# Attention units with the keys' two parts stacked, sample values as wide products, and the passages before both attentions re-ordered

## The chip, the cores and the metric

One core of a Trainium2 chip runs the whole kernel. The metric is the device time of one execution in microseconds (us); the kernel is timed in several runs, and the median counts. TensorE (PE) is the matrix engine, VectorE is DVE, ScalarE is ACT, GpSimd is POOL, and SyncE (SP) issues most of the DMAs.

## The reference

The reference is one inference step of a two-layer decoder, for a prompt of 512 tokens and for 8 sample tokens, each of which has 256 cached tokens behind it. Layer 0 runs dilated window attention (A, 8 heads of 64) beside gated linear attention (B, 4 heads, keys of 64 and values of 128). Layer 1 runs sparse attention (C, 16 query heads on 4 key heads), where an indexer picks 128 keys for a query. Every layer ends with a SwiGLU feed-forward part and a gated input embedding. Everything is float32.

```python
def ab_output(oa, ob, bog, li, prm):
    gate = jax.nn.silu(bog).reshape(*lead, B_HEADS, B_DV)
    ob = rmsnorm(ob, prm['b_out_norm'][li]) * gate
    o = jnp.concatenate([oa..., ob...], axis=-1)
    return o @ prm['w_out_ab'][li]
# A and C: QK-norm, scores + T5 bias, softmax over the keys of a dilated window (A)
s = jnp.einsum('btngd,btknd->btkng', qg, kg).reshape(bx, t, k, h) + bias
s = jnp.where(valid[..., None], s, -jnp.inf)
# C: the keys come from
score = jnp.where((key_pos[None, :] <= t[:, None])[None], index_scores(iq, iw, ik), -jnp.inf)
_, idx = lax.top_k(score, topk)
# every layer's end
x = x + (jax.nn.silu(hn @ w_ff1) * (hn @ w_ff3)) @ w_ff2
x = x + jax.nn.sigmoid(rmsnorm(x, g_ple) @ w_ple_gate) * (p_l @ w_ple_proj)
```

The kernel doesn't gather keys. It computes scores against all keys up to the end of the query block and adds a bias row that is very negative where a key is not allowed. In C the choice of the indexer is added as a mask of 0 and a very negative number.

## The kernel before, in words

Activations lie transposed: features on the 128 partitions, 520 token columns (512 of the prompt, 8 of the sample). A float32 product is made from rounded parts: `x = hi + lo`, and `hi*hi + lo*hi + hi*lo` are three matrix products at the fast rate. ACT makes the high part by a copy into a rounded type, POOL or DVE subtracts it to get the low part. Weights go by SP's DMA into a ring `w_raw`, ACT makes `w_hi` (L1315), POOL makes `w_lo` (L499).

The program on PE runs in this order: the input products of A and B (`products_in(0, ...)`), attention A, output products and feed-forward (`ffn(0)`), the input products of C, attention C, `ffn(1)`. Every engine has its own program in the order of the source; semaphores join them. No scheduler changes the order.

`attention` (PE L763 to L811, ACT L1387, DVE L1806) runs over units, one per pair of heads p, head of the pair `par`, and query block `qb`: 32 units in A, 64 in C. A unit of block qb is 128 x (128, 256, 384 or 512) scores. In step i of the loop PE makes the scores of unit i (L776: `q_hi*k_hi`, `q_hi*k_lo`, `q_lo*k_hi`, preceded in C by an addition of the mask, L774), turns unit i-3 (L785, transposes) and multiplies unit i-4 with the values (L797). DVE adds the bias while it leaves the accumulator and finds the largest (L1817), ACT takes the exponential, DVE scales by the sum (L1825), ACT copies the turned block. A head has 64 features, half of the 128 rows. So the tile `q_hi` or `q_lo` of one head holds the head in 64 rows and zeros in the other 64 (`zero_half`, by ACT), and the 128-row key tile holds the keys of both heads of the pair; the zeros cancel the other head. POOL makes these query tiles while attention runs (`split`/`place_a` L589 to L597 in A, `place_q_part` L653 in C).

Between the units lies other work, called from `between(i)`. In A (PE `sample_a`, L1100) it is the attention of the 8 sample tokens, one token in a step: scores against the cache at the steps `SCORES_A` (L1084: four products of 64 weight columns with 257 moved columns), values at the steps `VALUES_A` = 26 to 34 (L1096: eight products per token, each with 128 columns of the cached values as weights and two columns moved), the product for B's sample output (L1072: 16 products of two columns, before step 0's end), and the head norms of B (L1049).

The passage from products to attention: before unit 0 of A, PE transposes V (`attention_v` L1035, L1039) and DVE copies it out (L2027), ACT and DVE split the keys (L1587, L2024), POOL splits the queries and the keys of the next pair, and ACT and POOL split the weights of the feed-forward's first block (`high`, `low`), which stand in their queues ahead. Unit 0 waits for the last input block's accumulators to be free (`free_a`), since it uses the same banks. Before unit 0 of C, DVE splits the keys (L2169), makes the three masks from the top-k result (L2173), the sample's mask (L2175), and copies the causal block into the mask of query block 0 (L2176). PE waits for all of them.

## Time and profile before

| what | value |
|---|---|
| runs | 1574.65, 1575.99, 1582.1 us |
| median | 1575.99 us |
| the profiled execution's own time | 1581.09 us |
| its span in the trace | 1579.0 us |
| PE busy | 1532.3 us, 97 % |
| products of A and B | 0 to 201 us |
| passage and attention A | 201 to 321.9 us |
| ffn(0) | to 857 us |
| products of C | to 956.6 us |
| passage and attention C | 956.6 to 1082.7 us |
| ffn(1) | to the end |

### The profile page before, as it was taken

Reading aid. Unit: us, or ns where it says so; the run is one execution under the profiler, and the core shown is the slowest. Engines: PE = TensorE matmul, PEld = TensorE weight load, DVE = VectorE, ACT = ScalarE, POOL = GpSimd, SP = SyncE. Lnnn points to the kernel's source line nnn. Section 1 sums busy time; section 2 is a strip of 40 time slices with the busy share of each in tenths; the row PEclk is TensorE's granted clock in tenths of the full one; section 3 lists DMA queues with packets and bytes.
Section 4 is the critical chain, followed back from the end, with each engine's and each line's share of the span. In section 5 each row is a group of like instructions: output and inputs, shape, how many; then the busy total and the mean of one; then the engine's idle time right before and its main releaser. Section 6 shows DMA issues by size and latency. Waiting matters only on the chain.

```text
span 1579.0 us, 31089 instructions
## 1 busy us (share of the span) xinstructions
PE 1532.3 (97%) x12240; PEld 1477.4 (94%) x12240; DVE 684.8 (43%) x1172; ACT 657.3 (42%) x1094; POOL 682.5 (43%) x349
## 2 busy tenths in 40 slices
PE   7999989999999999999999998999999999999998
PEld 6999967999999999999989787999999999999998
DVE  4044446245443434221361696765633434432224
ACT  4242645324334343232463555653434343432234
POOL 3654643033444444444346465211444444444443
PEclk9999979689999999999999998999999999999999
DMA  5222433122332232333223321121322233323323
GB/s 171 88 95 63 142 116 113 67 67 81 94 91 87 87 93 93 94 106 93 93 86 119 106 77 68 56 86 43 92 82 92 93 93 93 93 94 95 105 93 121
DMA packets 52837, 146.92 MB, mean 93 GB/s; under 512 B 5485, under 2 KB 18057, under 8 KB 52250
## 3 DMA queue, kind: packets, MB, share of 16 engines
q1 hardware_dynamic: 50346, 137.17, 28.1%
q10 hardware_dynamic: 2416, 8.72, 1.5%
q8 instruction: 50, 0.82, 0.2%
q14 instruction: 25, 0.20, 0.0%
HBM read 139.11 MB, written 6.76 MB: 92 GB/s over the span
## 4 chain that ended last, share of the span: by engine, by line
PE 93%; DVE 4%; ACT 1%; issue 1%; DMA 0%; SPq 0%; ACTq 0%; DVEq 0%
PE PS L703 73%; PE PS L797 4%; PE PS L776 3%; DVE act_lo L1797 2%; PE PS L785 2%; PE PS L719 1%; PE PS L1096 1%; PE PS L1084 1%; PE PS L886 1%; PE PS L774 1%; PE PS L1162 1%; PE PS L1231 0%; DVE pp L1911 0%; PE PS L1072 0%; PE PS L1250 0%
## 5 line engine op out<-in xcount | busy, mean ns | idle before, releaser
L499 POOL TENSOR_TENSOR w_lo<-w_raw,w_hi 128x1024 fp32r<-128x1024 f32 x217 | 534.9, 2465 | 794.6 <-ACT w_hi L1315 794.6
L703 PE MATMUL PS<-act_hi,w_hi 128*128 128x260 f32 x2544 | 727.4, 286 | 14.5 <-POOL w_lo L499 10.0
L703 PE MATMUL PS<-act_lo,w_hi 128*128 128x260 f32 x2544 | 720.2, 283 | 0.0
L703 PE MATMUL PS<-act_hi,w_lo 128*128 128x260 f32 x2544 | 719.8, 283 | 0.0
L1315 ACT ACTIVATE w_hi<-w_raw 128x1024 fp32r<-128x1024 f32 x217 | 230.1, 1060 | 708.3 <-PE PS L703 704.6
L703 PEld LDWEIGHTS PS<-act_hi,w_hi 128*128 128x128 f32 x2544 | 480.5, 189 | 28.2 <-issue 21.3
L703 PEld LDWEIGHTS PS<-act_lo,w_hi 128*128 128x128 f32 x2544 | 480.9, 189 | 0.4
L703 PEld LDWEIGHTS PS<-act_hi,w_lo 128*128 128x128 f32 x2544 | 481.1, 189 | 0.0
L703 PE MATMUL PS<-h_hi,w_lo 128*128 128x260 f32 x704 | 198.8, 282 | 0.0
L703 PE MATMUL PS<-h_hi,w_hi 128*128 128x260 f32 x704 | 198.6, 282 | 0.0
L703 PE MATMUL PS<-h_lo,w_hi 128*128 128x260 f32 x704 | 198.5, 282 | 0.0
L703 PEld LDWEIGHTS PS<-h_hi,w_hi 128*128 128x128 f32 x704 | 132.6, 188 | 0.0
L703 PEld LDWEIGHTS PS<-h_lo,w_hi 128*128 128x128 f32 x704 | 132.3, 188 | 0.0
L703 PEld LDWEIGHTS PS<-h_hi,w_lo 128*128 128x128 f32 x704 | 132.2, 188 | 0.0
L1872 DVE TENSOR_TENSOR h_lo<-tmp,h_hi 128x520 f32 x44 | 83.8, 1905 | 40.1 <-ACT h_hi L1455 40.1
L1877 DVE TENSOR_TENSOR x<-PS,x 128x520 f32<-128x520 f32 x16 | 11.2, 700 | 176.5 <-PE PS L703 176.5
L1797 DVE SCALAR_TENSOR_TENSOR act_lo<-x,vecs,act_hi 128x520 fp32r<-128x520 f32 x48 | 74.3, 1567 | 24.4 <-ACT act_hi L1326 24.3
L1864 DVE TENSOR_TENSOR tmp<-PS,sq 128x520 f32<-128x520 f32 x44 | 30.8, 700 | 103.8 <-ACT sq L1451 103.8
L1404 ACT ACTIVATE tmp<-PS 128x128 f32<-128x128 f32 (+1 forms) x96 | 41.5, 433 | 77.3 <-PE PS L785 76.0
L1868 DVE TENSOR_TENSOR tmp<-PS,tmp 128x520 f32<-128x520 f32 x44 | 30.8, 700 | 95.4 <-PE PS L703 95.4
L1788 DVE TENSOR_TENSOR sqsum<-sqsum,sq 128x520 f32<-128x520 f32 x48 | 56.3, 1172 | 20.0 <-ACT sq L1321 19.0
L1862 DVE TENSOR_TENSOR tmp<-PS,nrs 128x520 f32<-128x520 f32 x44 | 30.8, 700 | 67.3 <-PE PS L703 67.3
(329 smaller groups left out, 1870.3 us busy)
## 6 DMA issues: line engine op xcount, KB each, us to landing
w_raw<-in_w SPq DMA_DIRECT2D x217, 512.0 KB, 3.5
kcA<-in_cache_k SPq DMA_DIRECT2D x8, 512.0 KB, 4.5
biasC<-scratch_rows SPq DMA_DIRECT2D x12, 256.0 KB
x<-in_xT SPq DMA_DIRECT2D x4, 520.0 KB, 5.9
out_y<-x SPq DMA_DIRECT2D x8, 260.0 KB, 4.5
vcA<-in_cache_v SPq DMA_DIRECT2D x4, 512.0 KB, 6.1
kcC<-in_pool_k SPq DMA_DIRECT2D x16, 128.0 KB, 2.5
vcC<-in_pool_v SPq DMA_DIRECT2D x16, 128.0 KB, 2.1
```

The source lines that it names most:

```text
L499: pool.tensor_tensor(w_lo[:, s, :], w_raw[:, s, :], w_hi[:, s, :].bitcast(F32), ALU.subtract).then_inc(S("w_lo"), 1)
L703: mm = pe.matmul(PS[:, 2 * place + half, 0:HALF], w[:, s, j * P:(j + 1) * P], r[:, c, cols], start=first and n == 0 and i == 0, stop=last ...
L776: mm = pe.matmul(PS[:, i % 2, 0:W], q_of[part][par][:, p % 2, qb * P:(qb + 1) * P], k[:, k_chunk(p), 0:W], start=n == 0 and not masked, st ...
L785: mm = pe.transpose(PS[:, 2 + i % 2, kb * P:(kb + 1) * P], ps[i % 3][:, kb * P:(kb + 1) * P], ident)
L797: mm = pe.matmul(PS[:, 4 + p % 2, qb * P:(qb + 1) * P], v_of(p, par, kb), pt[:, i % 2, kb * P:(kb + 1) * P], start=i % 8 == 0, stop=i % 8 ...
L1315: act.activation(w_hi[:, s, :], w_raw[:, s, :], ACT.Copy).then_inc(S("w_hi"), 1)
L1404: act.activation(pt[:, i % 2, 0:W], PS[:, 2 + i % 2, 0:W], ACT.Copy).then_inc(S("t_c"), 1)
L1788: dve.tensor_tensor(sqsum[:], sqsum[:], sq[:, m % 2, :], ALU.add).then_inc(S("ssum"), 1)
L1797: dve.scalar_tensor_tensor(act_lo[:, c, :], x[:, c, :], vecs[:, g:g + 1], act_hi[:, c, :].bitcast(F32), ALU.mult, ALU.subtract).then_inc(S ...
L1862: dve.tensor_tensor(halves(tmp[:, 1, :]), slot(0), halves(nrs[:]), ALU.mult).then_inc(S("f_a"), 1)
L1864: dve.tensor_tensor(halves(tmp[:, 1, :]), slot(0), halves(sq[:, 0, :]), ALU.mult).then_inc(S("free_v"), 1)
L1872: dve.tensor_tensor(h_lo[:, bass.ds(f, 1), :], tmp[:, 0:1, :], h_hi[:, bass.ds(f, 1), :].bitcast(F32), ALU.subtract).then_inc(S("h_lo"), 1)
```

## The change

It has four parts.

**Merged keys.** The key tile of head `par` now holds only that head: the high part in its own 64 rows and the low part in the other 64 (`act_hi` for par 0, `act_lo` for par 1). `q_hi` is copied into both halves (the second copy is called the twin), so one product gives `q_hi*k_hi + q_hi*k_lo`, and the second, with `q_lo` and zeros, gives `q_lo*k_hi`. Each of the 96 units has two score products instead of three. ACT's zeroing of `q_hi` goes; POOL gets one more copy per head (64 x 512), the key split is done by halves: two copies and two subtractions instead of one.

**Sample values of A.** The probabilities are scattered into a zeroed tile `pzA` (POOL zeroes, ACT scatters) that serves as weights of 64 columns; the cached values are moved, 512 columns at a time: two products per token, all into one accumulator, then one for the token's own value. DVE copies the result out at step 32 and four products of 16 columns pick each head's part at step 33. The tokens stand at steps 22, 23, 24, 26, 27, 28, 30, 31.

**Masks of C.** Query block 0 has no mask product: the causal part stands in the bias rows, whose right part is set to the very negative number by a memset instead of a product (`bias_rows`, L1931). PE waits for the mask of a query block at its first unit, not for all before unit 0. The sample's mask goes to DVE step 6.

**The passages.** Attention A makes scores in banks 2 and 3 and turns in 0 and 1, so unit 0 waits for one input block less. V is transposed in steps 0 and 1; the last head sum stands at step 2, B's sample output at steps 3 and 4, B's norms 3 to 4 steps later. The last block's weight splits leave the passage: `last_high` at ACT's step 6 (A) or 4 (C), `last_low` behind POOL's pair 1. The DVE steps for the sample's queries stand ahead of the state update.

```diff
-        NORMS_A = (4, 7, 11, 15, 18)
-        VALUES_A = (26, 27, 28, 29, 30, 32, 33, 34)
+        NORMS_A = (7, 10, 14, 18, 20)
+        VALUES_A = (22, 23, 24, 26, 27, 28, 30, 31)
+        def score_bank(base, i):
+            return (2 if base == BASE_A else 0) + i % 2
...
-                    low(n + (b0 + 2), (b0 + like) % 2)
+                    final = like == IN[l]["n"] - 1
+                    if not final:
+                        low(n + (b0 + 2), (b0 + like) % 2)
...
+            def split_q(pair, par):
+                hi, twin, lo, t = place_a(pair, par)
+                split_high(t, hi, twin)
+                split_low(hi, lo, t, "A_st")
+            def split_k(pair, par):
+                k = (act_hi, act_lo)[par]
+                hi, t = k[own[par], 4 + pair % 2, 0:SEQ], yA[own[par], Y_K + pair, 0:SEQ]
+                split_high(t, hi)
+                split_low(hi, k[other[par], 4 + pair % 2, 0:SEQ], t, "k_split")
...
+                elif part == 1:
+                    pool.tensor_copy(qC[0][par][other[par], p % 2, :], q).then_inc(S("C_st"), 1)
...
-                    if masked:
-                        pe.matmul(PS[:, i % 2, 0:W], identR[:], maskC[:, qb, 0:W], start=True, stop=False)
-                    for n, (part, k) in enumerate(((0, act_hi), (0, act_lo), (1, act_hi))):
+                    by_mask = masked and qb > 0
+                    if by_mask:
+                        if i < QB:
+                            pe.wait_ge(S("topk"), 1 + qb)
+                        pe.matmul(PS[:, score_bank(base, i), 0:W], identR[:], maskC[:, qb, 0:W], start=True, stop=False)
+                    k = (act_hi, act_lo)[par]
+                    for part in range(2):
+                        mm = pe.matmul(PS[:, score_bank(base, i), 0:W], q_of[part][par][:, p % 2, qb * P:(qb + 1) * P],
+                                       k[:, k_chunk(p), 0:W], start=part == 0 and not by_mask, stop=part == 1)
...
-            pe.wait_ge(S("free_a"), AB_BLOCKS + 2)
+            pe.wait_ge(S("free_a"), AB_BLOCKS + 1)
...
-                for t in range(4):
-                    for kb in range(2):
-                        c = t * NS + b
-                        mm = pe.matmul(PS[:, 7, 256 + 2 * c:258 + 2 * c], value_place(b)[:, kb, t * P:(t + 1) * P],
-                                       ptsA[:, kb, c:c + 33:32], start=kb == 0, stop=kb == 1)
+                for kb in range(2):
+                    c = P * b + 64 * kb
+                    mm = pe.matmul(PS[0:64, 7, :], pzA[:, c:c + 64], value_place(b)[:, kb, :],
+                                   start=b == 0 and kb == 0, stop=False)
...
+                if i < 2:
+                    attention_v(2 * i)
+                    attention_v(2 * i + 1)
+                elif i == 2:
+                    last_head_sum()
+                elif i < 5:
+                    sample_out_b(i - 3)
...
+            low_keys(0)
             for qb in range(1, QB):
                 dve.tensor_scalar(maskC[:, qb, 0:W], ...).then_inc(S("topk"), 1)
-            dve.tensor_scalar(sc8[:], wk8[:], GONE, NEG, ALU.not_equal, ALU.mult).then_inc(S("d_mask"), 1)
-            dve.tensor_copy(maskC[:, 0, 0:P], causal[:, SEQ - P:SEQ]).then_inc(S("topk"), 1)
+            low_keys(1)
+            dve.wait_ge(S("topk"), QB)
```

In the rows of the program's order, the first name after the arrow is the weights' or the first operand, the last figure the moved shape, and the brackets hold the semaphores that the instruction waits for. PE at the start of attention A, before: L1039 is the second half of V's transposes, L776 are scores, L1072 is B's sample output.

```order
L1039 MATMUL PS<-const,yA 128x128 [waits y_rs,A_v]
L1039 MATMUL PS<-const,yA 128x128 x3
L1039 MATMUL PS<-const,yA 128x128 [waits y_rs,A_v]
L1039 MATMUL PS<-const,yA 128x128 x3
L776 MATMUL PS<-act_hi,q_hiA 128x128 [waits k_split,A_st,t_x,A_zq,free_a]
L776 MATMUL PS<-act_lo,q_hiA 128x128
L776 MATMUL PS<-act_hi,q_loA 128x128
L1072 MATMUL PS<-qz,s 128x2 [waits A_v,s_new,s_qz]
L1072 MATMUL PS<-qz,s 128x2 x15
L776 MATMUL PS<-act_hi,q_hiA 128x256 [waits t_x]
L776 MATMUL PS<-act_lo,q_hiA 128x256
```

After, where L812 are scores and L1073 transposes V:

```order
L812 MATMUL PS<-act_hi,q_hiA 128x128 [waits k_split,A_st,t_x,A_zq,free_a]
L812 MATMUL PS<-act_hi,q_loA 128x128
L1073 MATMUL PS<-const,yA 128x128 [waits s_new,y_rs]
L1073 MATMUL PS<-const,yA 128x128 x3
L1073 MATMUL PS<-const,yA 128x128 [waits s_new,y_rs]
L1073 MATMUL PS<-const,yA 128x128 x3
L812 MATMUL PS<-act_hi,q_hiA 128x256 [waits t_x]
L812 MATMUL PS<-act_hi,q_loA 128x256
L1073 MATMUL PS<-const,yA 128x128 [waits A_v]
L1073 MATMUL PS<-const,yA 128x128 x3
L1073 MATMUL PS<-const,yA 128x128 [waits A_v]
L1073 MATMUL PS<-const,yA 128x128 x3
```

The 16 transposes, and their waits, now stand behind the scores of units 0 and 1, and B's sample output has left this place for steps 3 and 4.

PE at one step with a sample token's values, before (L785 turns, L797 multiplies by values, L1096 are the sample's values):

```order
L776 MATMUL PS<-act_hi,q_hiA 128x384 [waits t_x]
L776 MATMUL PS<-act_lo,q_hiA 128x384
L776 MATMUL PS<-act_hi,q_loA 128x384
L785 MATMUL PS<-const,sq 128x128 [waits t_c,t_n]
L785 MATMUL PS<-const,sq 128x128 x3
L797 MATMUL PS<-tmp,rs 128x128 [waits t_c]
L797 MATMUL PS<-tmp,rs 128x128 x2
L1096 MATMUL PS<-nrs,vcA 128x2 [waits values0,sm_pnc]
L1096 MATMUL PS<-nrs,vcA 128x2 x7
```

The same kind of step after (L821 turns, L833 multiplies by values, L1128 are the sample's values):

```order
L812 MATMUL PS<-act_lo,act_hi 128x384 [waits t_x]
L812 MATMUL PS<-act_lo 128x384
L821 MATMUL PS<-const,pA 128x128 [waits t_c,t_n]
L821 MATMUL PS<-const,pA 128x128 x3
L833 MATMUL PS<-tmp,vstA 128x128 [waits t_c]
L833 MATMUL PS<-tmp,vstA 128x128 x2
L1128 MATMUL PS<-vcA,yA 64x512 [waits values0,b_ln,sm_ptc]
L1128 MATMUL PS<-vcA,yA 64x512
```

Three score products have become two, and the eight products of two moved columns have become two of 512 columns.

DVE from the end of the top-k search to unit 0 of C, before (L2169 splits the keys, L2173 and L2175 make masks, L2176 copies the causal block, L1817 adds the bias of the first unit):

```order
L2169 TENSOR_TENSOR act_lo<-yC,act_hi 128x2x512 [waits k_hi,dve_chain]
L2173 TENSOR_SCALAR maskC<-xC 128x256
L2173 TENSOR_SCALAR maskC<-xC 128x384
L2173 TENSOR_SCALAR maskC<-workC 128x512
L2175 TENSOR_SCALAR sc<-wk 8x257
L2176 CAST maskC<-const 128x128
L1817 ISA xC,statC<-PS,biasC 128x128 [waits bias00,t_s]
```

After (L2227 are the halves of the key split, L2233 the masks, L1866 the bias of the first unit):

```order
L2227 TENSOR_TENSOR act_hi<-yC,act_hi 64x2x512 [waits k_hi,dve_chain]
L2233 TENSOR_SCALAR maskC<-xC 128x256
L2233 TENSOR_SCALAR maskC<-xC 128x384
L2233 TENSOR_SCALAR maskC<-workC 128x512
L2227 TENSOR_TENSOR act_lo<-yC,act_lo 64x2x512 [waits k_hi]
L1866 ISA xC,statC<-PS,biasC 128x128 [waits bias00,t_s,topk]
```

Two splits of 64 rows take the place of one, the sample's mask and the causal block have gone from here, and the first bias waits for the three masks.

## Rows read from the trace of the kernel before

**Rows 1.** Page: busy time of the span by engine; granted clock in 40 slices.

```profile
PE 1532.3 (97%) x12240; PEld 1477.4 (94%) x12240; DVE 684.8 (43%) x1172; ACT 657.3 (42%) x1094; POOL 682.5 (43%) x349
...
PEclk9999979689999999999999998999999999999999
```

**Rows 2.** Windows: stretch, length; PE, PEld, DVE, ACT, POOL busy; PEclk, DMA share, GB/s.

```profile
201.00:226.00 25.00, 18.95 (x91) 16.47 (x90) 15.05 (x33) 13.46 (x30) 15.13 (x16) 0.75 0.27 109
226.00:271.00 45.00, 43.76 (x242) 30.95 (x241) 26.80 (x72) 23.94 (x70) 14.68 (x16) 0.95 0.45 139
271.00:288.00 17.00, 16.43 (x123) 15.60 (x123) 8.78 (x40) 8.41 (x26) 0.00 (x0) 0.90 0.17 50
289.00:322.00 33.00, 33.00 (x152) 32.24 (x151) 6.05 (x18) 6.37 (x15) 0.00 (x0) 0.50 0.14 49
322.00:326.00 4.00, 4.00 (x19) 4.00 (x20) 1.90 (x7) 0.23 (x1) 0.00 (x0) 0.50 0.00 0
965.00:1083.00 118.00, 116.34 (x844) 107.26 (x843) 74.52 (x272) 72.41 (x220) 29.48 (x30) 0.97 0.20 65
```

**Rows 3.** Timeline of PE in attention C: start, duration, engine, line, operation, tiles, shapes.

```profile
968.25 0.31 PE L774 MATMUL PS<-maskC,identR 128*128 128x128 f32 x1
968.39 0.27 PE L776 MATMUL PS<-act_hi,q_hiC 128*128 128x128 f32 x1
968.50 0.27 PE L776 MATMUL PS<-act_lo,q_hiC 128*128 128x128 f32 x1
...
971.17 0.34 PE L776 MATMUL PS<-act_hi,q_hiC 128*128 128x384 f32 x1
971.35 0.34 PE L776 MATMUL PS<-act_lo,q_hiC 128*128 128x384 f32 x1
...
973.04 0.40 PE L776 MATMUL PS<-act_hi,q_hiC 128*128 128x512 f32 x1
973.28 0.39 PE L776 MATMUL PS<-act_lo,q_hiC 128*128 128x512 f32 x1
```

**Rows 4.** Chain of waits in attention A: start, duration, engine, line, instructions.

```profile
237.72 1.88 PE PS L1084 x8
...
284.31 1.68 PE PS L1096 x16
...
297.30 3.21 PE PS L1096 x16
```

**Rows 5.** Timeline of all engines in the passage to attention A.

```profile
196.97 1.32 POOL L512 TENSOR_TENSOR yA<-yA,rs 128x520 f32<-128x520 f32 x1
200.24 1.04 PE L719 MATMUL PS<-sq,const 128*128 128x260 f32 x4
201.12 1.04 PE L1039 MATMUL PS<-const,yA 128*128 128x128 f32 x8
205.40 0.30 PE L776 MATMUL PS<-act_hi,q_hiA 128*128 128x128 f32 x1 [1.58 <-DVE act_lo L2024]
206.50 6.90 PE L1072 MATMUL PS<-qz,s 128*128 128x2 f32 x32 [0.57 <-DVE vtokA L2027]
225.75 1.11 PE L1080 MATMUL PS<-sbA 33*64 33x257 f32 x2
```

**Rows 6.** Timeline of DVE in the passage to attention C.

```profile
954.79 1.62 DVE L2169 TENSOR_TENSOR act_lo<-yC,act_hi 128x1024 fp32r<-128x1024 f32 x1 [1.64 <-ACT act_hi L1731]
...
959.29 2.42 DVE L2175 TENSOR_SCALAR sc<-wk 8x257 f32<-8x257 f32 x1
963.18 0.29 DVE L1817 CUSTOM_DVE_ANT_0 xC<-PS,biasC 128x128 f32<-128x128 f32 x1 [1.33 <-PE PS L776]
```

**Rows 7.** Lines L660, L662, L1825: min/median/max ns, first and last start.

```profile
L660 POOL CAST q_hiC<-yC x16: 602/618/861, 934.9 to 1051.4; 64x512 fp32r<-64x512 f32 x16
L662 POOL TENSOR_TENSOR q_loC<-yC,q_hiC x16: 1254/1278/2132, 941.3 to 1052.1; 64x512 fp32r<-64x512 f32 x16
L1825 DVE TENSOR_SCALAR pC<-pC,statC x43: 285/420/1508, 964.7 to 1079.6; 128x128 f32<-128x128 f32 x11, 128x256 f32<-128x256 f32 x11, 128x512 f32<-128x512 f32 x11, 128x384 f32<-128x384 f32 x10
```

More of the change, by code:

```diff
@@ L650, in _ @@
                     place_v(pair, par)
+                if pair == 1:
+                    last_low(0)
+                elif pair == 2:
+                    pool.wait_ge(S("s_ks"), NS)
+                    pool.memset(pzA, 0.0).then_inc(S("sm_pz"), 1)
             ffn(0)
             def place_q_part(p, k):
-                par, part = k // 2, k % 2
+                par, part = k // 3, k % 3
                 if k == 0 and p >= 2:
@@ L1655, in _ @@
             attention(PAIRS_A, BASE_A, xsA, psA3, statA, sample_a)
+            act.wait_ge(S("sm_o"), 2)
+            for r in range(2):
+                rows = slice(HD * r, HD * r + HD)
+                act.activation(act_hi[rows, 0:4, SEQ:NT], sample_out_a(r), ACT.Copy).then_inc(S("sm_oh"), 1)
             act.wait_ge(S("t_s"), 32)
```

306 lines of the change are left out of this document (161 added, 145 removed).

## The prediction

> **What bounds the kernel now.** I read the page first: PE is busy 97% of the span, every other engine 43% or less [rows 1]. So a microsecond counts only if PE does less, waits less, or runs at a higher clock. Next I looked at the clock, since the same work costs twice the time at half of it. It is full in nearly all slices, but in slice 7 it is 0.6 and in the next 0.8 [rows 1], and those are the passage to attention A and attention A itself. The windows by stage say how much [rows 2]. A stretch of length L with mean clock c loses L x (1 - c) against full speed: 25 x 0.25 = 6.25 us in the passage, 45 x 0.05 = 2.25 and 17 x 0.10 = 1.7 in the middle of A, 33 x 0.50 = 16.5 in its last third, and 4 x 0.50 = 2.0 at the start of the feed-forward part. What PE did there matters: from 289 to 322 us it was busy 33.00 of 33.00 us, at half clock throughout. Then the timelines of PE in C and in the two passages [rows 3, 5, 6], where the start of one matmul to the start of the next is its cost, and the chain [rows 4] for the sample's products.
>
> **Merged keys.** It takes one score product of three from all 96 units. Start to start, such a product costs 968.50 - 968.39 = 0.11 us at 128 columns, 971.35 - 971.17 = 0.18 at 384, 973.28 - 973.04 = 0.24 at 512 [rows 3]; for 256 columns I take 0.12, between its neighbours. That is 0.65 us for four units, on PE's own path. C has 16 such fours: 10.4 us. In A 27 units lie behind the passage, which I count apart: 27 x 0.65 / 4 = 4.4 us.
>
> It adds work elsewhere. POOL makes a twin for each head: before, a pair of C costs it 2 x (0.618 + 1.278) = 3.8 us, now 2 x 0.618 = 1.24 more, 5.0 us [rows 7]. A pair lasts about 118 / 8 = 14.8 us, so POOL itself keeps up. The cover is this slack of two thirds; if it were gone, PE would wait for `C_st`. In A, pairs 2 and 3 have four POOL steps for the keys instead of two, and they are due a whole pair later. ACT copies the keys by halves, so twice at one price, as does DVE; both stand in the passages and are counted there. The zeroing of `q_hi` that ACT no longer does was off the path.
>
> **Masks of C.** The mask product of a 128-column unit costs 968.39 - 968.25 = 0.14 us [rows 3]; it goes 16 times: 2.2 us. In the passage to C the first bias starts at 963.18 [rows 6]. Before it DVE does the key split (1.62), three masks to 959.3, the sample's mask (2.42) and the causal copy (to about 961.9). Now the last two go and a second key split comes, of 64 rows and the same length, at 1.5: the DVE is through by 959.3 + 1.5 = 960.8 and PE, which only waits for the first key half, has the scores ready by then. The chain of units so starts 2.4 us earlier, and unit 2 a little more, since PE has less to do before it: 2.8. Bounds: 0.4, if the second ACT half makes the first split late by the length of the copy, and 4.
>
> So C brings 10.4 + 2.2 + 2.8 = 15.4 us if PE alone bounds it. It does so before: 116.34 busy of 118.00 us [rows 2]. But DVE and ACT are busy 74.5 and 72.4 us in it, and would be so in 103 us, at 72%. DVE's scaling of a block takes 420 ns in the median and up to 1508 [rows 7], the longest while POOL works, and POOL has 8 x 1.24 = 10 us more of work. A unit's chain (scores, bias, exponential, scaling, turn) has three units' time to run, and a stretched step uses up what is left of it. I take off 3 us, between nothing and 15 (each of the 14 added casts that fall into C stretches one scaling by 1508 - 420 ns = 1.1). C: 12.4 us.
>
> On this stretching, the Trainium skill ("SBUF — State Buffer", section "Who interferes with whom") says that DVE and GpSimd share a pair of ports as an exclusive lock, and that a `tensor_scalar` in two-port mode is fully blocked while GpSimd holds it. The spread of 285 to 1508 ns in rows 7 agrees, and L1825 is such an operation. By the rule alone, 14 casts of 0.618 us could block a scaling each for their whole length: 8.7 us instead of 3, and C's gain would be 6.7.
>
> **Passage to A.** From the end of the last head sum to the first sample scores PE takes 225.75 - 201.12 = 24.6 us [rows 5]. In it PE waits for V's copies, for the weights' splits that ACT and POOL do first, and 1.58 us for the key split; B's sample output takes 6.90 us at half clock. After, by my count, PE has 9.5 us of work there at full clock: the head sum 0.9, sixteen transposes 1.8 (8 in 0.9 by the rows), two scores products of six units 1.8, V's sample transposes 0.3, turns and value products of the first units 1.3, B's sample output 6.90 / 2 = 3.45. The keys can be copied as soon as POOL has finished y at 196.97 + 1.32 = 198.3: two ACT copies and two subtractions of DVE are through by 202.4, while PE already has unit 0. I add 2 us of waits: the sample scores start at 201.1 + 9.5 + 2.0 = 212.6, 13 us earlier. Bounds: 16 (no waits; the work at full clock), and 6 (half clock as before for all 9.5 us, less 2 of the waits).
>
> **Attention A from there.** Before, 322.0 - 225.75 = 96.2 us. Off: the three stretches at half clock, 2.25 + 1.7 + 16.5 = 20.4; the third product, 4.4. On: the norms of B that were in the passage (0.9); the values. A token's eight products cost 1.68 us at full clock [rows 4], two columns in 0.105 each record, all weight loading. Two products of 512 float32 columns are not in the trace; the nearest is L1084, four of 257 with 64 weight columns in 1.88 [rows 4], 1028 columns against 1024, so 1.87. That is 0.2 x 8, and 0.9 for the ninth: 2.5 us. Since I don't know that the clock stays up throughout, I put half of the passage's loss back for one more stretch, 3.1. Sum 96.2 - 20.4 - 4.4 + 0.9 + 2.5 + 3.1 = 77.9; A ends at 212.6 + 77.9 = 290.5, 31.5 us earlier.
>
> The 16.5 is the largest term, and it rests on what PE did: in 289 to 322 it was fully busy with two-column products at 0.50, and they ran at full clock, 1.68, at first. The products of 257 columns at 237.72 [rows 4] stand among the same units and ran at full clock, in a window of 0.95. So I take the half clock here to go with the two-column products back to back, and the new form has none in these steps.
>
> **The rest.** The feed-forward start is at full clock (+2.0 us), but waits for the split of mixed parts, which now have less time: -1.0. The deferred weight splits cost nothing, since the ring's next product is 80 us away; if the cover is gone, 2 x 2.5 us. POOL's memset of `pzA` and ACT's scattered copy lie in steps where both are under half busy: nothing.
>
> **Sum.** 31.5 + 1.0 + 12.4 = 44.9 us. The profiled execution took 1581.1, 5.1 us over the median of the runs; 1581.1 - 44.9 = 1536.2, and the same off the median 1531.1. I take the middle: 1534 us.
>
> **Rivals.**
> 1. The clock does not come back: half clock in the values' steps is set by something that the new form has as well. For it: PE was not idle before it fell. Against: the wide products of rows 4 at full clock. Gain less by 16.5: 1534 + 16.5 = 1550.5. The Trainium skill ("TensorE: Matmul & The Clock Gate", section "HAM oscillation — how this bites in real kernels") names idle gaps as what brings the clock down; by that, exchanging busy for busy changes nothing, as this rival has it. The row with 33.00 of 33.00 at 0.50 speaks against that rule as the only cause. 10%.
> 2. C turns to the DVE and ACT chain: each unit is bound by bias, exponential, scaling and turn, so the removed products only open gaps. For it: both at 72% with stretched steps. Against: PE at 98.6% of the stretch before. C then brings only its passage's 2.8 us instead of 12.4: 1534 + 9.6 = 1543.6. 18%.
> 3. The other side: C's clock falls. With a product or two less in each unit PE gets gaps, and where it had gaps before, 201 to 226, the clock was 0.75. At half clock for a share f of the 98 us or so that PE then has work, C costs 98 f more. It makes the kernel slower from 98 f > 44.9, f = 0.46; all of it gives 1534 + 98 = 1632. Against: C's clock was 0.97 with 98.6% busy, and it ran at full through waits of some tenths. 3%.
> 4. More than forecast, no stretch at half clock and no stretched steps in C: 3.1 + 3 + 3 less, about 1525. 7%.
>
> **How the numbers follow.** My forecast has 62% and, as the likeliest, gives the time: 1534. The rivals 1 and 2 reach 1551 and 1544; the bounds of the passage (+7, -3), of C's chain (+12, -3), of C's passage (+2.4, -1.2) and of the clock in A (-3.1) partly together give about +14 and -8; adding the two starting points (5 us) I take 1518 to 1551. Cases of both signs don't share the chance, so there is no second range. A measurement of this kernel can tell about 0.5%, 8 us: faster by more than that 95% (all but rival 3 and mishaps), within it 3%, slower 2%.
>
> **What would show it.** The changed trace should have: two scores products per unit with the same start-to-start times; the windows of the values' steps at a clock near 1.00 and their two products in some 1.87 us; the first sample scores at about 213 us; attention A's end at 290 to 291; C's first bias at 961, and C some 12 us shorter. I am wrong if the clock of the values' steps is 0.50 with wide products, if the first sample scores come after 218, or if PE in C has new gaps, ended by ACT or DVE, of more than 6 us in sum.

## The result, and the profile after

The changed kernel takes 1552.49 us in the median of 4 runs (1551.68 to 1554.47); the kernel before, beside it, 1575.32 us (4 runs, 1570.17 to 1582.10). The ratio is 0.9857 with a 95% interval of 0.9812 to 0.9902: faster by 22.8 us, where 42 were forecast (1576 to 1534). Measured again later it took 1548.3 us (6 runs) against 1571.72 (23 runs), ratio 0.9846, interval 0.9805 to 0.9887. The direction was that of the forecast, and most of the mechanisms were; its size was nearly double, and the median lies 1.5 us outside the stated range of 1518 to 1551 (the later one lies inside). Two executions of one variant took 2443 and 3012 us, far from all others, and are left out of all comparisons.

The page after, busy time and the granted clock in 40 slices, to be laid beside [rows 1]:

```profile
PE 1506.2 (97%) x12032; PEld 1438.8 (93%) x12032; DVE 686.9 (44%) x1172; ACT 654.1 (42%) x1093; POOL 701.3 (45%) x378
...
PEclk9999989999999999999999998999999999999999
```

The sixth digit of the clock, in the passage to attention A, was 7 and is 8; the eighth and ninth, before at the end of attention A and the start of the feed-forward part, were 6 and 8 and are 9. Windows of the changed kernel (stretch, length; busy time of PE, PEld, DVE, ACT, POOL; granted clock; DMA share; GB/s) answer to [rows 2]:

```profile
201.00:216.00 15.00, 13.44 (x82) 11.92 (x81) 10.35 (x30) 8.41 (x23) 11.41 (x14) 0.80 0.18 73
216.00:250.00 34.00, 33.27 (x170) 22.11 (x170) 15.57 (x45) 17.18 (x49) 15.62 (x18) 0.94 0.57 176
250.00:263.00 13.00, 9.60 (x59) 7.51 (x58) 10.77 (x26) 7.79 (x24) 11.29 (x13) 0.94 0.19 68
263.00:269.00 6.00, 6.00 (x22) 4.16 (x22) 4.13 (x14) 2.80 (x10) 0.00 (x0) 0.57 0.02 4
269.00:300.00 31.00, 30.98 (x152) 18.00 (x151) 12.13 (x42) 12.16 (x33) 0.00 (x0) 1.00 0.25 85
300.00:304.00 4.00, 3.33 (x26) 2.94 (x26) 2.55 (x6) 2.03 (x5) 0.00 (x0) 1.00 0.00 0
937.00:963.00 26.00, 18.28 (x94) 15.55 (x93) 16.72 (x45) 15.59 (x47) 16.55 (x15) 0.80 0.15 56
963.00:1053.00 90.00, 88.94 (x682) 82.44 (x681) 66.44 (x240) 59.10 (x180) 28.01 (x34) 1.00 0.22 69
```

The values' stretch, 269 to 300 us, runs at 1.00 where its predecessor ran at 0.50 from 289 to 322. Two stretches have more waiting than the forecast has: 250 to 263 (PE busy 9.60 of 13.00, DVE 10.77) and 937 to 963 (PE 18.28 of 26.00). The last row shows that C's units from the eleventh on are full: 88.94 of 90.00.

A line of the chain of waits in the changed kernel's attention A shows a token's values (start, duration, instructions), to be laid beside [rows 4]:

```profile
282.08 1.86 PE PS L1128 x4
```

1.86 us, against a forecast of 1.87.

To say where the time went, I divide each trace at the same instructions and count in each part the loss to the clock, length x (1 - granted clock), apart from the rest (the loss is counted while PE waits, too, where it costs less, so this division is approximate). For the kernel before it takes more than the one trace of the forecast, and the experiments below give five more. Means over the traces, in us (rest + clock loss):

| part | before, 6 traces | after, 2 traces | forecast gain | measured gain |
|---|---|---|---|---|
| products of A and B's end to sample scores | 18.3 + 7.2 | 13.0 + 1.9 | 13.0 | 10.6 |
| from there to the feed-forward part | 75.8 + 15.2 | 79.0 + 5.0 | 18.5 | 7.0 |
| passage to C and C's units 0 to 9 | 21.5 + 4.3 | 20.9 + 5.0 | 12.4, with the row below | -0.1 |
| C's other units and its end | 100.4 + 0.0 | 91.1 + 0.2 | | 9.1 |
| feed-forward parts, products of C | 1126.1 + 5.8 | 1126.0 + 6.3 | 1.0 | -0.4 |

The sum of the last column is 26; the runs say 23 to 24. The forecast's was 44.9. Four of the six traces before are of long executions (see the next section), so the measured gain by the clock is, if anything, on the large side.

### The profile page after: what moved, and what is told of

Read it like the earlier page. It is cut to its first block, busy times and chain, and to the rows that moved or that the text cites. A ratio compares the mean times of both kernels' runs of the same rounds, so it can differ in the third digit from the quotient of the medians.

```text
span 1552.7 us, 30718 instructions
## 1 busy us (share of the span) xinstructions
PE 1506.2 (97%) x12032; PEld 1438.8 (93%) x12032; DVE 686.9 (44%) x1172; ACT 654.1 (42%) x1093; POOL 701.3 (45%) x378
## 4 chain that ended last, share of the span: by engine, by line
PE 91%; DVE 4%; ACT 2%; issue 1%; DMA 1%; POOL 1%; SPq 0%; ACTq 0%; POOLq 0%; DVEq 0%
PE PS L735 75%; PE PS L833 3%; PE PS L812 2%; DVE act_lo L1846 2%; PE PS L821 2%; PE PS L751 1%; PE PS L1128 1%; PE PS L1116 1%; PE PS L1201 1%; PE PS L922 1%; PE PS L809 1%; ACT w_hi L1353 0%; PE PS L1271 0%; PE PS L1288 0%; DMA kcA<-in_cache_k 0%
## 5 line engine op out<-in xcount | busy, mean ns | idle before, releaser
L735 PE MATMUL PS<-act_hi,w_hi 128*128 128x260 f32 x2544 | 727.8, 286 | 15.2 <-POOL w_lo L508 10.1
L1926 DVE TENSOR_TENSOR x<-PS,x 128x520 f32<-128x520 f32 x16 | 11.2, 700 | 176.4 <-PE PS L735 176.4
```

Of the source, the lines that this page charges most:

```text
L735: mm = pe.matmul(PS[:, 2 * place + half, 0:HALF], w[:, s, j * P:(j + 1) * P], r[:, c, cols], start=first and n == 0 and i == 0, stop=last ...
```

## The experiments

**Five more executions of the kernel before.** The runs beside my variants had given a list of executions of the kernel before, and it shows what my three runs and one trace did not: two groups.

> The kernel before, unchanged, looked at once more. Its 34 executions beside the variants so far fall in two groups: 1564 to 1575 us at a mean clock of 0.980 to 0.989, and 1578 to 1584 at 0.975 to 0.980. If the groups differ by the long half-clock stretch of the sample values (288.5 to 326 us in the profile that I predicted from), an execution of the first group has that stretch at full clock, or a good part of it, with everything else alike. If the stretch at half clock is in every execution and the groups differ by something else, it stands there in this trace too.

> The kernel before, unchanged. If the execution is of the shorter group (1564 to 1575 us), my theory expects that the half-clock stretch from 288.5 to 326 us is absent or much shorter, and the rest alike; the rival expects it there, and another stretch gone.

Of the five, three took 1581 to 1584 us and two 1566.94 and 1570.60. In the three long ones the stretch at half clock under the sample values is there again as in [rows 2], 288.6 to 326.1, 287.0 to 324.5 and 289.4 to 326.9 us. In the shortest one, the kernel and its instructions being the same, windows and chain read:

```profile
288.00:321.00 33.00, 33.00 (x243) 32.52 (x243) 10.81 (x26) 8.09 (x18) 2.39 (x1) 0.84 0.22 69
289.00:301.00 12.00, 12.00 (x105) 11.78 (x106) 4.06 (x12) 3.54 (x9) 0.00 (x0) 1.00 0.33 119
302.00:307.00 5.00, 5.00 (x24) 4.78 (x23) 0.95 (x2) 1.58 (x3) 0.00 (x0) 0.50 0.00 0
```

```profile
295.77 1.68 PE PS L1096 x16
...
301.13 2.33 PE PS L1096 x16
```

The two-column products ran at full clock until 302 us, 1.68 us a token, and PE was busy throughout here too. The clock loss of attention A was 4.6 us in this trace, 11.2 in the one of 1570.60 and 18 to 21 in the four long ones, while the rest of A is 75.4 to 76.3 us in all six, and the clock loss outside A is 15 to 19 us in all six. The 56 executions of the kernel before that stand beside my variants have no trace, but they fit: 29 took 1564 to 1575 us and 27 took 1577 to 1584; mean span x (1 - clock) is 23.8 us in the first group and 36.7 in the second, and mean span x clock is 1542.4 and 1542.0. The 16.5 us that I took from one trace are thus real, but about one execution of two is of that kind. My theory held, the rival (another stretch) fell.

**Only the form of the values, in the kernel before.**

```diff
-                for t in range(4):
-                    for kb in range(2):
-                        c = t * NS + b
-                        mm = pe.matmul(PS[:, 7, 256 + 2 * c:258 + 2 * c], value_place(b)[:, kb, t * P:(t + 1) * P],
-                                       ptsA[:, kb, c:c + 33:32], start=kb == 0, stop=kb == 1)
+                for kb in range(2):
+                    mm = pe.matmul(PS[0:64, 7, :], ptsA[:, kb, :], value_place(b)[:, kb, :],
+                                   start=kb == 0, stop=kb == 1)
```

> The kernel before, with only the sample values of A changed in form: two products of 64 weight columns and 512 moved ones per token instead of eight with two moved columns (into the same accumulator, so that the sample's output is not the right one). If the half clock from 288.5 to 326 us goes with the two-column products, it is full there and attention A ends 15 us earlier (16.5 + 2.0 for the clock, less 1.5 to 3 for the products). If the clock stays at half there, as my first rival had it, A ends 3 to 4 us later.

Window of this kernel over the values:

```profile
270.00:304.00 34.00, 34.00 (x171) 20.75 (x170) 12.19 (x44) 13.57 (x38) 0.00 (x0) 0.99 0.24 78
```

The clock is 0.99 (and 1.00 from 304 to 308 us, where the feed-forward part starts), and PE is as busy as before, 34.00 of 34.00. The feed-forward part starts at 303.56 us instead of 321.88 in the profile before; 2.6 of these 18.3 us lie in the passage, and attention A from the sample scores on takes 80.4 instead of 96.1 us, 15.8 less, as expected. In the runs it is 1564.94 us (10 runs, 1559.88 to 1566.19) against 1571.72, ratio 0.9943, interval 0.9911 to 0.9975: 7 to 9 us, since half of the executions before had no long stretch. Its runs spread over 6 us, those of the kernel before over 20. The rest of A grew by 2.9 us (78.7 against 75.8): the wide form is dearer in work than the 1.6 that I gave its eight tokens, and pays by the clock. A check without the clock in it: at full clock, from the first token's values to the eighth's, the narrow form took 21.65 us in the shortest trace (279.48 to 301.13) and the wide form 23.53 (276.16 to 299.69), so 1.9 for seven tokens; 7 x 0.18 = 1.3 of it are the values' own products.

**The reverse: narrow values in the changed kernel.**

```diff
-                for kb in range(2):
-                    c = P * b + 64 * kb
-                    mm = pe.matmul(PS[0:64, 7, :], pzA[:, c:c + 64], value_place(b)[:, kb, :],
-                                   start=b == 0 and kb == 0, stop=False)
+                for t in range(4):
+                    for kb in range(2):
+                        c = P * b + 64 * kb
+                        mm = pe.matmul(PS[:, 7, 128 * t:128 * t + 2], value_place(b)[:, kb, t * P:(t + 1) * P],
+                                       pzA[:, c:c + 2], start=kb == 0, stop=kb == 1)
```

> The changed kernel with its sample values of A put back to eight products per token with two moved columns and 128 weight columns (into one accumulator, so the sample's output is not the right one), at the new steps. If the half clock goes with these products, the stretch from about 269 to 295 us is at 0.50 and A is 12 to 16 us longer; if it was the state of the rest of the kernel before, A is 1.5 us shorter (1.68 against 1.86 us per token, eight times).

> The changed kernel with the two-column sample values again, for a trace: in its timed runs it lost about 28 us to the clock, against 16 to 19 of the kernels with wide values beside it, at 2.5 us less of work. If the two-column products bring the clock down, steps 22 to 31 (about 265 to 295 us) have a stretch at 0.50 longer than 3.4 us, which no trace with wide values has there.

Four runs took 1555.5 to 1559.2 us, with 25 to 30 us lost to the clock; the three kernels with wide values measured beside them took 1547.6 to 1552.3 in the median and lost 15 to 19 in the mean. Windows of one more execution:

```profile
269.00:282.00 13.00, 13.00 (x62) 12.90 (x62) 3.33 (x13) 2.83 (x9) 0.00 (x0) 0.50 0.41 134
283.00:289.00 6.00, 6.00 (x55) 5.86 (x54) 1.78 (x8) 2.03 (x7) 0.00 (x0) 1.00 0.30 111
289.00:296.00 7.00, 7.00 (x35) 6.90 (x35) 3.43 (x12) 3.75 (x11) 0.00 (x0) 0.52 0.00 1
```

Half clock at 269 to 282 and 289 to 296 with PE busy throughout, full between. Clock loss in A is 18.0 us against 1.7 to 6.8 in the ten traces with wide values, the rest 76.0 against 79.0: the narrow form is 3 us cheaper in work and 11 to 16 dearer by the clock. A as a whole takes 94.0 us here against 84.5 and 83.4 in the two traces of the changed kernel: 10 to 11 longer, where 12 to 16 were expected. The rival of this expectation (a state of the rest of the kernel) fell. What stays open is which part of the form does it: the narrow form has two moved columns instead of 512, and also 16 records of 128 weight columns in a token instead of four of 64; the two swaps change all of it together.

**The third score product put back.**

```diff
-                    for part in range(2):
+                    for n, part in enumerate((0, 1, 1)):
...
-                                       k[:, k_chunk(p), 0:W], start=part == 0 and not by_mask, stop=part == 1)
+                                       k[:, k_chunk(p), 0:W], start=n == 0 and not by_mask, stop=n == 2)
```

> The changed kernel with a third score product put back in each of the 96 units (q_lo times the key tile is added twice, so the scores differ a little). If PE alone bounds the units, it costs 0.65 us for four units, 24 times: 15.6 us, 10.4 of them in C. If attention after the change were bound by the chain over DVE and ACT (my rival 2), much of it would be hidden: under 6 us in C.

1559.9 us (10 runs) against 1548.3 of the changed kernel beside it: 11.6 us. In the trace A is 5.0 us longer without the clock's part, and C from unit 10 to unit 62 (counted from 0) is 7.3 us longer, against a forecast of 8.5 for these 52 units. PE does bound the units. Without the clock's part the whole is 14.4 us longer, so the forecast of 15.6 was near; 3 of it came back because these runs lost less to the clock (13.4 us in the mean against 16.8).

**POOL's twin left out.**

```diff
+                if pair < 2:
                     split_high(t, hi, twin)
+                else:
+                    split_high(t, hi)
...
                 elif part == 1:
-                    pool.tensor_copy(qC[0][par][other[par], p % 2, :], q).then_inc(S("C_st"), 1)
+                    if p < 2:
+                        pool.tensor_copy(qC[0][par][other[par], p % 2, :], q).then_inc(S("C_st"), 1)
+                    else:
+                        pool.sem_inc(S("C_st"), 1)
```

> The changed kernel without POOL's second copy of q_hi from the third pair on, in A and in C (the other half of the tile keeps old values, so the scores of these pairs are wrong). It takes 12 casts of 0.6 us out of C and 4 out of A. If POOL's added work stretches DVE's steps and so costs what I took off for it, C is 3 us shorter or more; by the trace, where C's units after the eighth run at PE's own rate, C changes by less than 1 us, and A between 250 and 262 us by 1 to 2 us.

1549.3 us (4 runs) against 1548.3. Without the clock's part, unit 10 to 62 of C takes 83.7 us, 83.2 in the changed kernel, and A from the sample scores on 79.0 in both, so the 1 to 2 us expected there didn't come either. Its window over C's later units:

```profile
960.00:1049.00 89.00, 87.54 (x670) 81.09 (x669) 64.20 (x236) 58.07 (x178) 19.96 (x20) 1.00 0.21 66
```

POOL is busy 19.96 us instead of 28 (the window of 963 to 1053 above), and PE still 87.54 of 89.00. The added casts cost nothing that can be measured; the 3 us that I took off for them were wrong. So was my estimate of 8.7 by the rule of the Trainium skill ("SBUF — State Buffer", section "Who interferes with whom"). The trace agrees with the rule for single instructions: in C of the changed kernel, 25 scalings (L1874) beside which POOL works take 755 ns in the mean, the 39 others 390. But C doesn't get longer by it.

**DVE's steps out of the passage to C.** DVE in the changed kernel's passage to C (start, duration, line, operation), to be laid beside [rows 6]:

```profile
936.12 1.62 DVE L2227 TENSOR_TENSOR act_hi<-yC,act_hi 64x1024 fp32r<-64x1024 f32 x1 [1.61 <-ACT act_hi L1778]
937.76 1.52 DVE L2233 TENSOR_SCALAR maskC<-xC 128x256 fp32r<-128x256 f32 x2
939.20 1.51 DVE L2233 TENSOR_SCALAR maskC<-workC 128x512 fp32r<-128x512 f32 x1
940.74 2.18 DVE L2227 TENSOR_TENSOR act_lo<-yC,act_lo 64x1024 fp32r<-64x1024 f32 x1
942.96 0.29 DVE L1866 CUSTOM_DVE_ANT_0 xC<-PS,biasC 128x128 f32<-128x128 f32 x1
```

The first bias starts 6.2 us after the products' end at 936.75; before it was 7.75 (963.18 - 955.43). PE starts unit 0's scores at 937.94 and then waits. Of the five steps ahead of the bias (the second row holds two), the mask of query block 3 and the second key split are needed only by later units.

```diff
             low_keys(0)
-            for qb in range(1, QB):
...
-            low_keys(1)
-            dve.wait_ge(S("topk"), QB)
+            mask(1)
+            mask(2)
+            dve.wait_ge(S("topk"), QB - 1)
...
-                if i == 6:
+                if i == 0:
+                    mask(3)
+                elif i == 1:
+                    low_keys(1)
+                elif i == 6:
```

> The changed kernel with two DVE steps taken out of the passage to C: the mask of query block 3 stands behind unit 0's bias, the second key split behind unit 1's. The first bias then starts 3.7 us earlier (1.5 + 2.2). Since the two steps come back between the first units, I expect 1 to 3 us less in all. The rival: the head sum and the half clock that follows the wait set the time of unit 2, and the gain is under 0.5 us.

The second of these kernels has, beside this, ACT's `last_high_c()` at step 14 instead of 4 and POOL's `last_low(1)` behind pair 2 instead of 1.

> The changed kernel with both DVE steps out of the passage to C (as before) and ACT's and POOL's split of the feed-forward's second weight block moved from C's step 4 and pair 1 to step 14 and pair 2. In the first units of C, PE waits for ACT, which there does the last head's norm, this split (1.05 us), the value copies and the sample's queries. If ACT is what bounds these units, they are 1 us shorter than with the DVE steps moved alone, and 1 to 2 us shorter than in the changed kernel. The rival (a fixed point behind, the sample's queries, which wait for something else) expects no difference.

DVE in the first of these kernels:

```profile
930.96 1.62 DVE L2227 TENSOR_TENSOR act_hi<-yC,act_hi 64x1024 fp32r<-64x1024 f32 x1 [1.62 <-ACT act_hi L1778]
932.61 1.52 DVE L2232 TENSOR_SCALAR maskC<-xC 128x256 fp32r<-128x256 f32 x2
934.16 0.29 DVE L1866 CUSTOM_DVE_ANT_0 xC<-PS,biasC 128x128 f32<-128x128 f32 x1
934.38 1.20 DVE L2232 TENSOR_SCALAR maskC<-workC 128x512 fp32r<-128x512 f32 x1
...
936.84 1.22 DVE L2227 TENSOR_TENSOR act_lo<-yC,act_lo 64x1024 fp32r<-64x1024 f32 x1
```

The bias starts 2.6 us after the products' end (at 931.60), 3.6 us sooner, as expected. Windows from the products' end to unit 8, in this order of the kernel before, the changed one, this one, and the second one with the weight split moved too:

```profile
955.43:974.80 19.37, 13.66 (x75) 12.00 (x74) 13.42 (x36) 11.80 (x33) 13.41 (x10) 0.82 0.03 10
936.75:956.29 19.54, 13.26 (x65) 11.29 (x63) 14.25 (x35) 11.94 (x33) 10.39 (x10) 0.74 0.04 13
931.60:947.64 16.04, 11.89 (x64) 9.79 (x63) 12.65 (x35) 11.76 (x33) 10.38 (x10) 0.89 0.05 17
934.99:951.04 16.05, 11.91 (x65) 9.81 (x63) 13.08 (x35) 10.93 (x32) 10.39 (x10) 0.89 0.04 16
```

PE is idle 5.7 us before, 6.3 after, 4.15 with the two DVE steps moved, and 4.14 with the weight split moved as well. So the DVE steps gave 2.1 us of waiting, and moving ACT's split took away none: the rival of that expectation isn't excluded. From the products' end to the end of attention C it takes 114.7 us in the first kernel and 113.1 in the second, against 116.4 and 117.8 in the two traces of the changed kernel. The clock loss in it is 3.4 and 1.7 us against 5.1 and 5.1, so the 1.6 us between the first and the second are one stretch of 3.4 us at half clock less, seen in one trace of each. The whole: 1547.61 us (6 runs) and 1546.11 us (6 runs), ratio to before 0.9827 (0.9780 to 0.9874) and 0.9797 (0.9758 to 0.9837); beside the second, nine of the eleven executions of the kernel before were of the long group, which makes its ratio look better than it is.

**POOL's addition ahead of the query split, and all together.**

```diff
-                    if after_low:
+                    if after_low and not final:
                         after_low(like)
                     if q is not None:
                         add_eps(l, q, nrs[:] if final else sq[:, q % 2, :], n)
+                    if after_low and final:
+                        pool.wait_ge(S("sq_e2"), q + 1)
+                        after_low(like)
```

> The changed kernel with POOL's addition for the last head sum ahead of the query split of head 1, instead of behind it. In the passage to A PE waited at 204.5 and 205.6 us for it; it comes about 2.5 us earlier. I expect the sample scores 1 to 2 us earlier, unless the query split is then late for unit 4, in which case nothing. If the half clock from 210.1 comes from these waits, it goes too, and another 3 to 5 us with it.

> The changed kernel with all edits to the passages together: POOL's addition for the last head sum of A ahead of the query split, the two DVE steps of C among the first units, the weight split of C at step 14. Work at full clock was 1529 to 1530 us in each alone. If they add up, it is 1 to 2 us less than the changed kernel in work at full clock and 2 to 4 us less in time; the clock's share varies by more than that.

The first took 1552.29 us (1544.64 to 1552.74, four near 1552 and two near 1545), so no gain: PE's wait of 0.75 us for the addition is gone and the one for V's copy is 0.44 instead of 0.74 us, but a new one of 1.23 stands before unit 1's value products. The passage without the clock's part is 0.5 us shorter (12.6 against 13.1), and the clock fell as before, although those waits were shorter. The combination took 1545.34 us (6 runs, 1543.81 to 1549.88), ratio 0.9819, interval 0.9772 to 0.9867. Without the clock's part it is 1528.5 us in the mean against 1529.9 of the changed kernel's ten runs. It is the fastest median, but its interval overlaps that of the changed kernel (0.9805 to 0.9887); what I would trust is the 2.1 us less of waiting in the passage to C, which stand in all three traces of these kernels (PE idle 4.1 us against 5.5 to 6.3 in the seven traces with the old order there). Attention C is 3 to 4 us shorter in them, the rest of it by the clock; in span x clock of the runs (1529.9 and 1529.3 us for the two kernels before this one) it doesn't show.

**Ten more products at the feed-forward part's start.**

```diff
+                        if extra and half == 0 and n == 0:
+                            for _ in range(extra):
+                                pe.matmul(PS[:, 2 * place, 0:HALF], w_hi[:, s, j * P:(j + 1) * P], hi[:, c, cols],
+                                          start=True, stop=True)
                         for i, (w, r) in enumerate(((w_hi, hi), (w_hi, lo), (w_lo, hi))):
```

> The changed kernel with ten more products of 260 columns at the start of the first feed-forward part (their results are overwritten): 1.2 us of work that delays everything behind it. If the same waits are followed by a half-clock stretch or not by when they fall, stretches after the waits at 350.3, 797.8 and 1101.8 us come or go, and the time changes by 1.2 us and multiples of about 1.7. If the program fixes them, all stretches move by 1.2 us and the time is 1.2 us longer.

Inconclusive as designed: 1547.75 us (4 runs) with a spread of 1541.55 to 1552.24, more than the change of phase that it was to show. But its trace shows something else. Its passage to A and attention A are the changed kernel's, instruction for instruction, with the same two waits of 0.7 and 0.8 us, and no half clock follows:

```profile
200.00:211.00 11.00, 9.44 (x71) 8.04 (x70) 8.57 (x28) 6.76 (x19) 7.70 (x10) 1.00 0.06 25
```

The sample scores start 12.9 us after the products' end, against 15.6 and 13.7 in the two traces of the changed kernel, and this is the execution of 1541.55. What the run was meant to show stands in the other traces. PE waits 3.3 us for the norm at the start of C's products in every trace. Windows of 11 us around this wait, of the kernel before, of another execution of it, and of the changed kernel:

```profile
819.00:830.00 11.00, 7.75 (x64) 7.54 (x64) 6.86 (x8) 5.44 (x9) 5.03 (x2) 1.00 0.41 119
```

```profile
820.00:831.00 11.00, 7.89 (x45) 7.89 (x46) 6.28 (x7) 4.86 (x8) 4.89 (x2) 0.69 0.39 122
```

```profile
797.00:808.00 11.00, 7.75 (x42) 7.54 (x41) 7.40 (x8) 6.05 (x10) 3.86 (x2) 0.69 0.36 117
```

PE's busy time is 7.75, 7.89 and 7.75 us of 11, and the clock 1.00, 0.69 and 0.69. The same kernel with the same wait keeps the clock once and loses 3.4 us another time. So whether a stretch follows a wait differs from execution to execution of one kernel, and the stretches that stand in the changed kernel's first trace and not in the one before (353.5, 800.6, 1104.4 us) are no effect of the change: in its second trace the first and the last are gone, and the clock loss outside attention was 5.8 us before and 6.3 after in the mean.

## Why the prediction was wrong

**Failed: the clock in the last third of A.** "33 x 0.50 = 16.5 in its last third", and from it "Off: the three stretches at half clock, 2.25 + 1.7 + 16.5 = 20.4". The mechanism was right: the long half clock goes with the two-column form of the values, and in the wide form it is gone (experiments in both directions). The size was taken from one execution, which was among the long ones: 1581.09 us, 5.1 over a median of three runs. That distance was in front of me, and I halved it at the end as if it were noise of the same kind as everything else. It was the term itself: A's clock loss is 15.2 us in the mean of six traces, 4.6 to 20.8 in single ones. After it is 5.0, where I had 3.1. Forecast gain by the clock in A 17.3, measured 10.2: 7 of the missing 19 us.

**Failed: the work in A.** I forecast 1.0 us less work and waiting between the first sample scores and A's end; it is 3.2 more. The third product brought 5.0 (forecast 4.4). Against it stand the values, 2.9 dearer in their eight tokens by the kernel with only their form changed, and 1.1 in what finishes them (forecast 2.5 for both; the ninth product and the four that pick the heads take 1.00 and 0.99, where the kernel before had L1132, 1.81 at half clock), the norms 0.9 as forecast, and waits that I didn't have: steps 16 to 21, between the sample's scores and values, hold few products beside the units to fill PE, while DVE has B's norms and the sample's softmax and POOL the last pair. The chain there:

```profile
251.95 1.02 DVE yA L2109
253.00 0.04 DVE yA L2111
253.04 1.53 issue
254.56 0.41 DVE small L1964
...
257.97 0.03 DVE nrs L2137
258.00 1.10 issue
259.11 0.67 DVE xA L1866
```

The longest wait there, from the timeline of the changed kernel, and one DVE step of the sample's softmax in the kernel before (L2080) and in the changed one (L2137):

```profile
261.36 0.61 PE L1081 MATMUL PS<-small,const 128*128 128x32 f32 x2 [2.16 <-ACT s L1655]
...
271.55 0.25 DVE L2080 TENSOR_SCALAR nrs<-const,nrs 64x64 f32<-64x64 f32 x1
...
257.97 1.22 DVE L2137 TENSOR_SCALAR nrs<-const,nrs 64x64 f32<-64x64 f32 x1
```

The steps of B's norm (L2109, L2111) and of the sample's softmax (L1964 to L2137) stand between the biases (L1866) that PE waits for; "issue" is the rest of L2111 and L2137. PE is idle 3.4 us of 250 to 263, and in 216 to 250 another 0.7 for keys that come by DMA, 4.1 in all; before it was 1.8 in all of 226 to 288 [rows 2]. The gap between scores and values isn't new (before it was steps 16 to 25), and it isn't the removed score product that covered the waits: with the third product put back, PE is idle 4.4 us there. New is that the last norms of B, the softmax and POOL's last pair lie in the same steps; the step shown took 0.25 us before, with POOL idle, and takes 1.22 beside POOL. No run moved these steps apart, so this cause is argued, not shown. With these 2.3, about 1 us of the difference isn't assigned.

**Mis-sized: the passage to A.** 10.6 of 13.0. Without the clock's part it is 13.0 us from the end of the products to the sample scores, and I had 12.5 with the waits, so that part stands; but the clock still falls, for 10.2 us from 210.1 in one trace and for 6.8 from 213.6 in the other: "9.5 us of work there at full clock" was not what happened in either (it is what happened in the one trace of the run with ten more products, 12.9 us in all). Timeline of the changed kernel, to be laid beside [rows 5]:

```profile
203.27 1.25 PE L1073 MATMUL PS<-const,yA 128*128 128x128 f32 x8 [0.74 <-DVE vtokA L2088]
204.19 1.29 POOL L528 TENSOR_TENSOR nrs<-nrs,sqsum 128x520 f32<-128x520 f32 x1
205.63 1.12 PE L751 MATMUL PS<-nrs,const 128*128 128x260 f32 x4 [0.75 <-POOL nrs L528]
...
207.59 1.84 PE L1103 MATMUL PS<-qz,s 128*128 128x2 f32 x16
210.49 3.41 PE L1103 MATMUL PS<-qz,s 128*128 128x2 f32 x16
215.96 1.11 PE L1112 MATMUL PS<-sbA 33*64 33x257 f32 x2
```

PE waits 0.74 and 0.75 us, for V's copy and for POOL's addition, and B's sample output, also of two columns, runs half at half clock: its 16 records last 1.84 at 207.59 us and 3.41 at 210.49. One reading of the prediction is off by two slices: of the clock's 40 digits [rows 1] it gives the 6 and the 8 to the passage and attention A, but they lie at 276 to 355 us, and the passage is the 7 before them. No term rests on it, since the terms come from the windows.

**Right in its later units, wrong in its beginning: C.** Unit 10 to unit 62 took 92.5 us in every trace before and 83.2 after, without the clock's part. The mask products of these two units in the kernel before (L774) and in the changed one (L809):

```profile
982.06 0.53 PE L774 MATMUL PS<-maskC,identR 128*128 128x384 f32 x1
...
1074.53 0.44 PE L774 MATMUL PS<-maskC,identR 128*128 128x384 f32 x1 [0.18 <-DVE statC L1817]
...
962.00 0.53 PE L809 MATMUL PS<-maskC,identR 128*128 128x384 f32 x1
...
1045.19 0.44 PE L809 MATMUL PS<-maskC,identR 128*128 128x384 f32 x1 [0.53 <-DVE statC L1866]
```

9.3 us of a forecast 10.3 for these units (2.0 of it the masks, by the kernel with the third product, which takes 90.5; my estimate for them was 1.8). Rival 2, a bound by the chain, fell for these units. But from the products' end to unit 10 it gained nothing (25.8 and 25.9 us in the mean), where I had 2.8 for the passage and 2.1 for these units: DVE's second key split took 2.18 us instead of 1.5, and PE is idle 6.3 us up to unit 8 where it was 5.7, so the first units are bound by DVE's and ACT's steps, not by PE, and neither the missing product nor the missing mask counts in them. The same split takes 1.22 us where POOL is idle beside it (moved behind unit 1, see the experiments). The 3 us taken off for contention covered part of that by luck.

**Right: no stretches at half clock in C's units from the eleventh on, no effect of POOL's casts, nothing in the feed-forward parts** (1126.1 + 5.8 before, 1126.0 + 6.3 after). My 1.0 for the start of the feed-forward part is inside what single traces differ by. Rival 1 (clock stays) gave nearly the measured time, 1550.5, and for the wrong reason: the clock came back. None of the three signs that I had named for being wrong appeared (wide products at 0.50, sample scores after 218 us, new gaps of over 6 us in C); what did was attention A's end at 300 us instead of 290 to 291, and no sign that I had named watched the size of the clock term.

## What to carry to other kernels

Before a term is read off a trace, look whether the executions of the kernel fall in groups, and in which of them the trace lies: a profiled execution that is above the median of the runs has something in it that the others haven't, and the largest clock term is the first suspect. A saving per instruction holds where PE is the bound (C's later units), and must be set to nothing where other engines' steps stand in the chain (the first units behind a passage). A term that a step costs on one engine should be read where the other engines work as they will after the change: the second key split took 2.18 us beside POOL and 1.22 without it. And where the clock differs from execution to execution, two variants should be compared by their waits and by span x clock too, not by medians alone.

## What the runs showed of the hardware

- The same program has two groups of times, 1564 to 1575 and 1577 to 1584 us, with 1542 us of span x clock in both. In the six traces the difference is how long TensorE runs at 1.2 GHz in attention A, most of it while it does the two-column products of the sample values among those of the units, without a pause (33.00 of 33.00 us busy at 0.50 in one execution, 12.00 of 12.00 at 1.00 in another).
- Products of 512 float32 columns with 64 weight columns take 0.93 us each (1.86 for two), and with them TensorE stayed at 2.4 GHz in the same place: 0.99 from 270 to 304 us in the kernel before with them, 1.00 from 269 to 300 in the changed one.
- A wait of 3.3 us is followed by a stretch at half clock in some executions (0.69 in 11 us) and by none in others (1.00).
- A `tensor_tensor` of DVE on 64 rows x 1024 took 1.62 and 2.18 us in the passage to C while POOL worked beside it, and 1.22 us where POOL was idle; on 128 rows, with POOL at work, it took 1.62 [rows 6]. So beside POOL, half the rows saved nothing; no run has 128 rows without POOL.
